# Rotary queries from two expanded tiles with mixed halves, in place of four tiles of which two are half-swapped copies

## The chip, the cores and the metric

The kernel runs on one core of a Trainium2 chip. The metric is the device time of one execution in microseconds (us). TensorE multiplies matrices, VectorE (DVE in the profile) and ScalarE (ACT) work elementwise, GpSimd (POOL) does a few elementwise steps, and SyncE (SP) issues every transfer of this kernel, in program order. PEld is TensorE's loading of a stationary operand, which overlaps the multiplication before it.

## The reference

One layer of a streaming encoder: 2048 prompt tokens and 64 sample tokens, width 1024. The part that is touched is the query side of the latent attention, with 8 heads of 64 plain and 32 rotary columns:

```
q = (rmsnorm(cq, g_q) @ w_uq).reshape(b, t, MLA_HEADS, MLA_NOPE + MLA_ROPE)
q_nope = q[..., :MLA_NOPE]
q_pe = rope(q[..., MLA_NOPE:], pos)

def rope(x, pos):            # half = 16
    x1, x2 = x[..., :half], x[..., half:]
    return jnp.concatenate([x1 * cos - x2 * sin, x1 * sin + x2 * cos], axis=-1)
```

Everything is float32. The kernel splits each operand into a high and a low part and forms three products (high by high, high by low, low by high).

## The kernel before

**Stages.** `project_inputs` comes first (to about 356 us), then window attention with the first loads of latent attention, latent attention, and the output projection with the gated feed-forward part (from about 1000 us to the end). All engines meet at the end of `project_inputs`, SyncE after its last stores have landed; the later stages overlap at their borders.

**`project_inputs`.** The 2112 tokens are cut into five blocks (`BLOCKS`) of 424 columns (the last has 416). In each block, ten weight tiles (step j = 0 to 9, chunk t = 10 b + j) are multiplied with the block's normalised input: 24 products a chunk into one of two accumulators `acc`. VectorE reads each accumulator out, times the inverse root (`product_times_rstd`), and TensorE may start chunk t when `acc_free` says that chunk t - 2 is read. Weights arrive as 512 KB transfers into three raw slots (`load_w`, L249); ScalarE makes the high part (`w_hi_of`, L412), VectorE the low part (`w_lo_of`, L546). During block b the input of block b + 1 is loaded (`load_x`, L245) and split by ScalarE (L438) and VectorE (L551).

**Expansions.** The latent vectors of block b are expanded during block b + 1, by a list: `after[j]` names the items that TensorE computes behind chunk j, and the other engines handle the same items in the same order. A block has 14 items: four of plain queries ("nope"), two of rotary queries ("rope", items 4 and 5, behind chunks 2 and 3), four of keys, four of values. Block 4's items come together at the end (`last_expansions`), then those of the old cache. Products go to four banks `ex`; `ex_done` counts products, `ex_free` counts banks that VectorE has read. The results pass through a ring of four slots; SyncE stores each slot (`keep`, L323 for values, L326 for the rest), and the slot is free when its store has landed (`ring_out`).

**A rotary item.** Item i covers four heads. TensorE expands it twice, once with its columns in order and once with the two halves of each head swapped (the host appends the swapped copy to `w_head`): 2 x 6 products. VectorE multiplies the first with the cosines and the second with the signed sines (`turn`), adds them (`turned`), and later forms the low part (`rope_low`). The eight 128-column tiles of weights for this (four by two row halves) are loaded by `more_wx(1)` in four transfers and split in one piece by `wx_hi_of(1)` and `wx_lo_of(1)`, in block 0.

**Order on SyncE around `more_wx(1)`.** In block 0 it comes behind step 4's weight load; then the rotary key, the query store (`stored`), the next weight tile, and in step 5 `keep_bias` with its eleven transfers, and the next query store. VectorE reuses a staging tile only when its query store has landed.

**Window attention.** SyncE runs a loop over 128-token tiles (`step`, L969). A step issues, in this order: the next tile's loads (L930 to L932), the spread of the reciprocals (L914), the output store (L920), a slice of values (L978), then on odd tiles `head_keys` (L954, L956) and on even tiles `head_queries` (L947, L948), which bring the first head of latent attention piece by piece, and last `keep`, the store of the reciprocals (L961). VectorE overwrites the output tile only after its store has landed (`att_out`). Tiles 4 to 11 are in a rolled loop, the others written out; tile 14 calls `head_queries` twice.

**Latent attention** loads each later head in rows of 16 (`load`, L1493).

Of the kernel before, what the change touches and what calls it, by code (L numbers as in the profile page):

```python
# [17 lines left out]
ALU = mybir.AluOpType  # L18
ACT = mybir.ActivationFunctionType
F32 = mybir.dt.float32  # L20
# [45 lines left out]
def project_inputs(nc, d, early):  # L66
# [4 lines left out]
    with ExitStack() as ctx:  # L71
# [8 lines left out]
        RING = 4  # L80
        NX = 24
        w_raw = sb("pi_w_raw", [P, RAWS, KD, P])
# [103 lines left out]
        OLD = [("old key", i) for i in range(4)] + [("old value", 0)]  # L186
        BANKS = 16
        after = [[0, 1], [2, 3], [4], [5, 6], [7], [8, 9], [10, 11], [12, 13], [], []]

        def bank(b, e):  # L190

            return BANKS * b + e + max(0, min(e - 4, 2))

# [33 lines left out]
        def _(sp):  # L227
# [46 lines left out]
            def wx(lo, hi):  # L274
                return wx_raw[:, lo:hi].rearrange("p a (h c) -> p (a h) c", h=2 if hi - lo == 4 else 4)

# [3 lines left out]
            def more_wx(part):  # L280
                sp.wait_ge(wx_split, part)
                for m in range(2 if part == 1 else 0):
                    sp.dma_start(wx(2 * m, 2 * m + 2), head_cols(m * P + NOPE, m * P + NOPE + ROPE)).then_inc(wx_in, 16)
                    sp.dma_start(wx(4 + 2 * m, 6 + 2 * m), head_cols(m * P + NOPE + ROPE, m * P + P)).then_inc(wx_in, 16)
                if part == 2:
                    sp.dma_start(wx(0, 4), head_cols(2 * P, 2 * P + NOPE)).then_inc(wx_in, 16)
                    sp.dma_start(wx(4, 8), head_cols(2 * P + NOPE, 2 * P + NOPE + V_DIM)).then_inc(wx_in, 16)
# [18 lines left out]
            def keep(b, e):  # L306

                kind, i = item(b, e)
                _, slot, _ = place(b, e)
                rows, n = width(b, e)  # L310
                if kind == "rope":
                    sp.wait_ge(turn_lo, 2 * b + i + 1)
                else:
                    sp.wait_ge(ex_free, bank(b, e) + 1)
                c0 = cols(b)[0] if b < BLOCKS else TOK
                if kind == "nope":
                    to = d["qn_scr"][i * P:(i + 1) * P, :, c0:c0 + n]
                elif kind == "rope":
                    to = d["qr_scr"][i * P:(i + 1) * P, :, c0:c0 + n]
# [84 lines left out]
        def _(act):  # L404
# [68 lines left out]
            def wx_hi_of(s):  # L473
                act.wait_ge(wx_in, (32, 96, 128)[s])
                act.activation(wx_hi[:, 8 * s:8 * s + 8], wx_raw[:], ACT.Copy).then_inc(wx_hi_made, 1)
                if s == 2:
                    act.wait_ge(old_in, 32)
                    act.activation(old_kpe[64:96, 1].bitcast(F32R), old_kpe[64:96, 0], ACT.Copy).then_inc(wx_hi_made, 1)
                    act.activation(old_hi[:], old_raw[:], ACT.Copy).then_inc(wx_hi_made, 1)
# [57 lines left out]
        def _(dve):  # L537
# [30 lines left out]
            def split_low(b, e):  # L568
# [11 lines left out]
                if kind == "rope":  # L580
                    if i == 0:
                        dve.wait_ge(rope_in[b % 2], 64 * (b // 2 + 1))
                    first = bank(b, e)
                    if 2 * b + i:
                        dve.wait_ge(turn_done, 2 * b + i)
                    for part in range(2):
                        dve.wait_ge(ex_done, first + part + 1)
                        dve.tensor_tensor(turn[:, part, 0:n], ex[:, (first + part) % 4, 0:n],
                                          rope[:, b % 2, part, 0:n], ALU.mult).then_inc(ex_free, 1)
                    if i == 1:  # L590
                        rope_low(b, 0)
# [25 lines left out]

            def wx_lo_of(s):
                dve.wait_ge(wx_hi_made, s + 1)
                dve.tensor_tensor(wx_lo[:, 8 * s:8 * s + 8], wx_raw[:], wx_hi[:, 8 * s:8 * s + 8].bitcast(F32),  # L620
                                  ALU.subtract).then_inc(wx_split, 1)
# [85 lines left out]
        def _(pe):  # L707
# [19 lines left out]
            def expand(b, e):  # L727
                kind, i = item(b, e)
                rows, n = width(b, e)
                if e == 0:  # L730
# [3 lines left out]
                    if b < BLOCKS:  # L734
                        pe.wait_ge(lat_split, 3 * b + 3)
                at = bank(b, e)
                for part in range(2 if kind == "rope" else 1):
                    if at + part >= 4:
# [4 lines left out]
                    elif kind == "rope":  # L743
                        mm = from_queries(out, 8 + 4 * part + i, 2, n)
                    elif kind == "key":
                        mm = three(out, wx_hi[:, 16 + i], wx_lo[:, 16 + i], lat_hi[:, 2, 0:n], lat_lo[:, 2, 0:n])
                    elif kind == "old key":
                        mm = three(out, wx_hi[:, 16 + i], wx_lo[:, 16 + i], old_hi[:], old_lo[:])
                    else:
                        vw_hi = wx_hi[:, 20:24].rearrange("p a c -> p (a c)")  # L750
                        vw_lo = wx_lo[:, 20:24].rearrange("p a c -> p (a c)")
                        if kind == "value":
# [53 lines left out]
def window_attention(nc, d, ahead, early, ctx, first_ctx, ps):  # L806
# [116 lines left out]
    def sync(sp, first_row):  # L923
# [301 lines left out]
def latent_attention(nc, d, ahead, mix, ctx, rooms, ps, wa, own):  # L1225
# [220 lines left out]
    def sync(sp):  # L1446
# [46 lines left out]
        def load(i, p, s):  # L1493
# [3 lines left out]
            if s in PIECE_AT:  # L1497
# [117 lines left out]
    def tensor(pe, begin):  # L1615

        def max_chunk(i, p, pos, m):
# [3 lines left out]
            if pos == 0 and m == 0:  # L1621
                pe.wait_ge(ahead["in"], 16 * 5 * 8)
                pe.wait_ge(ahead["head_in"][p], QK_DMAS * 16 * (i + 1))
# [890 lines left out]
def encoder_layer(nc, d):  # L2514
    for name, shape in (("bias_far", (P, HEADS, 2 * P)), ("qn_scr", (HEADS * NOPE, 2, TOK)), ("qr_scr", (HEADS * ROPE, 2, TOK)),
                        ("kn_scr", (HEADS * NOPE, 2, KEYS)), ("kpe_scr", (ROPE, 2, KEYS)), ("vt_scr", (KEYS, HEADS * V_DIM))):
# [172 lines left out]
```

## Time and profile before

| | us |
|---|---|
| median of 3 runs | 2764.75 |
| lowest and highest of the runs | 2761.0, 2767.46 |
| span of the profiled execution | 2765.2 |
| projections, end of the stage | about 356 |
| TensorE busy over the span | 2665.2 |
| VectorE busy over the span | 1904.3 |
| ScalarE busy over the span | 1425.0 |
| GpSimd busy over the span | 478.9 |

The profile page gives the busy time of each engine; the timeline lists instructions in order of time with the idle time before each and what ended it; the view of waits sums such idle times by waiting line and releaser. Of SyncE only the issues of transfers are listed.

### The profile page before, as it was taken

To read this page: it belongs to the slowest core of one execution; us is meant where nothing else is said; L and a number is where in the kernel's file an instruction comes from. 1 tells how busy PE (TensorE), PEld (TensorE's weight loads), DVE (VectorE), ACT (ScalarE), POOL (GpSimd) and SP (SyncE) were. 2 spreads that over 40 slices of the span, in tenths; PEclk is the share of its full clock that TensorE was granted. 3 is DMA by queue.
4 is the path that set the end of the run, shared out by engine and by line. 5 is a ranking of instruction groups with operands and counts; after the bars stand their busy time and mean duration, and the time that the engine had idled before them with its cause. 6 is when DMAs were issued, how large, how long until landed. Compare 5 with 4: busy or idle time off the path is not lost.

```text
span 2765.2 us, 45010 instructions
## 1 busy us (share of the span) xinstructions
PE 2665.2 (96%) x13603; PEld 2433.1 (88%) x13603; DVE 1904.3 (69%) x2793; ACT 1425.0 (52%) x3042; POOL 478.9 (17%) x401
## 2 busy tenths in 40 slices
PE   8999978899999998999999999999999999999997
PEld 7999844677777787999999999999999999999997
DVE  6877667788778846877478754687546875468743
ACT  5444367577666754644355443554435544356532
POOL 1111041244433441100100022000220002200001
PEclk9999999899999999999999999999999999999999
DMA  7666655444545242343334433345333443334332
GB/s 221 218 212 230 215 154 157 85 83 75 91 85 88 68 165 85 113 137 120 113 100 140 162 114 115 100 139 164 121 106 102 139 163 118 116 102 135 118 121 88
DMA packets 181775, 357.73 MB, mean 129 GB/s; under 512 B 50692, under 2 KB 119780, under 8 KB 180324
## 3 DMA queue, kind: packets, MB, share of 16 engines
q1 hardware_dynamic: 181636, 356.00, 43.7%
q8 instruction: 72, 1.18, 0.2%
q14 instruction: 67, 0.55, 0.1%
HBM read 301.28 MB, written 55.43 MB: 129 GB/s over the span
## 4 chain that ended last, share of the span: by engine, by line
PE 71%; DVE 6%; issue 3%; SPq 2%; DMA 2%; ACT 2%; POOL 1%; DVEq 0%; ACTq 0%; POOLq 0%
PE mf_acc L2214 55%; PE at_ps L1640 6%; PE at_ps L1626 2%; PE at_ps L1659 2%; PE at_ps L1662 2%; PE at_ps L1660 2%; DVE la_part L1741 1%; DVE mix_w_lo L2392 1%; DMA room<-in_w_up 1%; ACT mix_w_hi L2273 1%; DMA att_scr<-wa_outT 1%; DVE la_low L1438 1%; SPq L920 0%; SPq L914 0%; PE mf_st L2255 0%
## 5 line engine op out<-in xcount | busy, mean ns | idle before, releaser
L2392 DVE TENSOR_TENSOR mix_w_lo<-room,mix_w_hi 128x1024 fp32r<-128x1024 f32 (+1 forms) x338 | 471.3, 1395 | 528.6 <-ACT mix_w_hi L2273 527.3
L2214 PE MATMUL mf_acc<-mix_a_hi,mix_w_hi 128*128 128x424 f32 (+1 forms) x2016 | 721.2, 358 | 12.7 <-DVE mix_w_lo L2392 5.0
L2214 PE MATMUL mf_acc<-mix_a_hi,mix_w_lo 128*128 128x424 f32 (+1 forms) x2016 | 715.3, 355 | 0.0
L2214 PE MATMUL mf_acc<-mix_a_lo,mix_w_hi 128*128 128x424 f32 (+1 forms) x2016 | 713.8, 354 | 0.0
L2273 ACT ACTIVATE mix_w_hi<-room 128x1024 fp32r<-128x1024 f32 (+1 forms) x338 | 383.1, 1134 | 491.7 <-PE mf_acc L2214 479.1
L2214 PEld LDWEIGHTS mf_acc<-mix_a_hi,mix_w_hi 128*128 128x128 f32 x2016 | 379.5, 188 | 28.2 <-DVE mix_a_lo L2446 6.0
L2214 PEld LDWEIGHTS mf_acc<-mix_a_hi,mix_w_lo 128*128 128x128 f32 x2016 | 379.8, 188 | 11.3
L2214 PEld LDWEIGHTS mf_acc<-mix_a_lo,mix_w_hi 128*128 128x128 f32 x2016 | 379.8, 188 | 9.6 <-issue 0.7
L2214 PE MATMUL mf_acc<-mf_h_hi,mix_w_hi 128*128 128x424 f32 (+1 forms) x944 | 339.3, 359 | 3.0 <-DVE mf_h_lo L2483 1.4
L2214 PE MATMUL mf_acc<-mf_h_hi,mix_w_lo 128*128 128x424 f32 (+1 forms) x944 | 335.7, 356 | 0.0
L2214 PE MATMUL mf_acc<-mf_h_lo,mix_w_hi 128*128 128x424 f32 (+1 forms) x944 | 335.1, 355 | 0.0
L1640 PE MATMUL at_ps<-ahead_q,ahead_k 96*128 96x512 f32 (+8 forms) x1008 | 259.0, 366 | 0.0
L1698 ACT ACTIVATE la_prob<-at_ps 128x512 f32<-128x512 f32 (+1 forms) x336 | 175.5, 522 | 156.8 <-PE at_ps L1640 146.7
L2163 POOL TENSOR_TENSOR mf_ss<-mf_sq,mf_ss 128x424 f32<-128x424 f32 (+1 forms) x105 | 141.9, 1351 | 547.6 <-ACT mf_sq L2299 315.8
L1741 DVE TENSOR_REDUCE la_part<-at_ps 128x1 f32<-128x512 f32 (+4 forms) x328 | 188.8, 594 | 60.3 <-PE at_ps L1626 58.3
L1640 PEld LDWEIGHTS at_ps<-ahead_q,ahead_k 96*128 96x128 f32 (+2 forms) x1008 | 180.7, 192 | 37.5 <-issue 0.4
L2214 PEld LDWEIGHTS mf_acc<-mf_h_hi,mix_w_hi 128*128 128x128 f32 x944 | 178.1, 189 | 10.4 <-DVE mf_h_lo L2483 2.5
L2214 PEld LDWEIGHTS mf_acc<-mf_h_lo,mix_w_hi 128*128 128x128 f32 x944 | 178.0, 189 | 6.2 <-issue 1.7
L1438 DVE TENSOR_TENSOR la_low<-la_prob,la_high 128x512 fp32r<-128x512 f32 (+3 forms) x227 | 158.8, 706 | 33.9 <-ACT la_high L1699 29.6
L2214 PEld LDWEIGHTS mf_acc<-mf_h_hi,mix_w_lo 128*128 128x128 f32 x944 | 178.0, 189 | 4.6
L1699 ACT ACTIVATE la_high<-at_ps 128x512 fp32r<-128x512 f32 (+1 forms) x336 | 174.2, 519 | 0.0
L2464 DVE SCALAR_TENSOR_TENSOR mf_cv<-mf_u,mf_conv_w,mf_cv 128x424 f32<-128x424 f32 (+1 forms) x220 | 151.3, 688 | 32.6 <-DVE mf_cv L2461 25.7
(207 smaller groups left out, 4074.8 us busy)
## 6 DMA issues: line engine op xcount, KB each, us to landing
room<-in_w_up SPq DMA_DIRECT2D x220, 512.0 KB, 3.6
room<-in_w_down SPq DMA_DIRECT2D x80, 704.0 KB, 4.1
pi_w_raw<-in_w_in SPq DMA_DIRECT2D x49, 512.0 KB, 6.1
room<-in_w_out SPq DMA_DIRECT2D x40, 512.0 KB, 3.6
la_rec_all<-inv_scr SPq DMA_DIRECT2D x32, 256.0 KB
ahead_k<-kn_scr SPq DMA_DIRECT2D x28, 280.0 KB, 5.5
ahead_q<-qn_scr SPq DMA_DIRECT2D x28, 264.0 KB, 5.1
room<-in_x SPq DMA_DIRECT2D x4, 1696.0 KB, 11.7
```

The lines of the kernel that those rows point to most:

```text
L1438: eng.tensor_tensor(low[0:keys, x % RING, off:n], prob[0:keys, x % RAWS, off:n], high[0:keys, x % RING, off:n].bitcast(F32), ALU.subtract) ...
L1626: pe.matmul(sx[0:rows, (NCH * p + first_chunk[pos] + m) % 2, 0:n], q[0:MR, p, 0, q0:q0 + rows], k[0:MR, p, 0, c0:c0 + n], start=True, stop ...
L1640: mm = pe.matmul(out, k[0:rows, p, a, c0:c0 + keys], q[0:rows, p, b, n0 + off:n0 + n], start=(term == 0), stop=(term == 2))
L1659: pe.matmul(out, v[0:keys, p, vt, 0:V_LO.start], hi, start=(m == 0), stop=False, skip_group_check=True)
L1698: act.activation(prob[0:keys, x % RAWS, off:n], sc[0:keys, x % 4, off:n], ACT.Exp, scale=MLA_SCALE)
L1699: act.activation(high[0:keys, x % RING, off:n], sc[0:keys, x % 4, off:n], ACT.Exp, scale=MLA_SCALE).then_inc(exp_done, 1)
L1741: dve.tensor_reduce(part[0:rows, parity(p, pos), t, slot:slot + 1], sx[0:rows, bank, 0:n], AX_X, ALU.max).then_inc(sx_free, 1)
L2163: pool.tensor_tensor(ss[:, kind, 0:n], sq[:, slot, 0:n], zeros[:, 0:n] if first else ss[:, kind, 0:n], ALU.add).then_inc(sq_added, 1)
L2214: mm = pe.matmul(acc[:, t_bank[0], 0:n], w[:, g, k], x[:, k, 0:n], start=(first and k == 0 and m == 0), stop=(last and k == count - 1 and ...
L2273: act.activation(w_hi[:, g, 0:count], w_raw[:, g, 0:count], ACT.Copy).then_inc(w_hi_made, 1)
L2392: dve.tensor_tensor(w_lo[:, g, 0:count], w_raw[:, g, 0:count], w_hi[:, g, 0:count].bitcast(F32), ALU.subtract).then_inc(w_split, 1)
L2464: dve.scalar_tensor_tensor(out=out, in0=u[:, g, 1:n + 1], scalar=conv_w[:, 1, bass.ds(f, 1)], in1=out, op0=ALU.mult, op1=ALU.add).then_inc ...
```

## The change

The two halves x1 and x2 of each head's rotary columns are laid into two tiles. Tile A holds x1 of the even heads and x2 of the odd heads; tile B holds x2 of the even heads and x1 of the odd heads. Each has 8 heads by 16 rows = 128 rows. With C the cosines and S the signed sines (minus for even heads' rows, plus for odd ones'), A C + B S is the first half of the even heads' result and the second half of the odd heads'; B C - A S is the other. So item 4 computes both tiles (2 x 6 products, behind chunk 2), item 5 computes none on TensorE, and VectorE multiplies the same two banks again for item 5; the banks are freed then. What else changes with it:

- `more_wx(1)` issues eight transfers of 16-column pieces of four heads in place of four of 32-column pieces of eight heads; 4 weight tiles are split in place of 8 (`WX`, `NX`).
- `BANKS`, the number of banks a block uses, is 14 in place of 16.
- `qr_scr` is laid out by halves. `head_queries` therefore issues two transfers for the rotary rows (16 rows each) in place of one (32 rows), eight more in all; the later heads' loads keep their number and size.

```diff
-        NX = 24
+        NX = 20
+        WX = ((0, 8), (8, 12), (12, 20))
...
-            return BANKS * b + e + max(0, min(e - 4, 2))
+            return BANKS * b + e
...
+            def half_turns(m, tile, odd):
+
+                at = m * P + NOPE + (ROPE // 2 if tile != odd else 0)
+                to = wx_raw[:, 2 * tile + m].rearrange("p (h e c) -> p h e c", e=2, c=ROPE // 2)[:, :, odd]
+                return to, d["w_head"][odd::2, :, at:at + ROPE // 2].rearrange("h p c -> p h c")
...
                 for m in range(2 if part == 1 else 0):
-                    sp.dma_start(wx(2 * m, 2 * m + 2), head_cols(m * P + NOPE, m * P + NOPE + ROPE)).then_inc(wx_in, 16)
-                    sp.dma_start(wx(4 + 2 * m, 6 + 2 * m), head_cols(m * P + NOPE + ROPE, m * P + P)).then_inc(wx_in, 16)
+                    for tile in range(2):
+                        for odd in range(2):
+                            sp.dma_start(*half_turns(m, tile, odd)).then_inc(wx_in, 16)
...
             def wx_hi_of(s):
-                act.wait_ge(wx_in, (32, 96, 128)[s])
-                act.activation(wx_hi[:, 8 * s:8 * s + 8], wx_raw[:], ACT.Copy).then_inc(wx_hi_made, 1)
+                a, z = WX[s]
+                act.wait_ge(wx_in, (32, 160, 192)[s])
+                act.activation(wx_hi[:, a:z], wx_raw[:, 0:z - a], ACT.Copy).then_inc(wx_hi_made, 1)
...
-                    first = bank(b, e)
+                    first = bank(b, 4)
...
-                    for part in range(2):
-                        dve.wait_ge(ex_done, first + part + 1)
-                        dve.tensor_tensor(turn[:, part, 0:n], ex[:, (first + part) % 4, 0:n],
-                                          rope[:, b % 2, part, 0:n], ALU.mult).then_inc(ex_free, 1)
+                    for half in range(2):
+                        part = half ^ i
+                        dve.wait_ge(ex_done, first + half + 1)
+                        dve.tensor_tensor(turn[:, part, 0:n], ex[:, (first + half) % 4, 0:n],
+                                          rope[:, b % 2, part, 0:n], ALU.mult).then_inc(ex_free if i else turn_parts, 1)
                     if i == 1:
                         rope_low(b, 0)
-                    dve.wait_ge(ex_free, first + 2)
+                        dve.wait_ge(ex_free, first + 2)
+                    else:
+                        dve.wait_ge(turn_parts, 2 * b + 2)
                     dve.tensor_tensor(turned[:, i, 0:n], turn[:, 0, 0:n], turn[:, 1, 0:n],
-                                      ALU.add).then_inc(turn_done, 1)
+                                      ALU.subtract if i else ALU.add).then_inc(turn_done, 1)
...
+                if kind == "rope" and i == 1:
+                    return
...
-                        mm = from_queries(out, 8 + 4 * part + i, 2, n)
+                        mm = from_queries(out, 8 + 2 * part, 1, n)
...
-            sp.dma_start(ahead["q"][NOPE:NOPE + ROPE, 0, :, cols].bitcast(F32),
-                         d["qr_scr"][0:ROPE, :, cols]).then_inc(ahead["in"], 16)
+            for e in range(2):
+                rows = slice(NOPE + ROPE // 2 * e, NOPE + ROPE // 2 * (e + 1))
+                sp.dma_start(ahead["q"][rows, 0, :, cols].bitcast(F32),
+                             d["qr_scr"][e, 0:ROPE // 2, :, cols]).then_inc(ahead["in"], 16)
...
-                                 d["qr_scr"][bass.ds(h * ROPE, ROPE)][r:r + 16]).then_inc(ahead["head_in"][g], 16)
+                                 d["qr_scr"][(m - 4) ^ g, bass.ds(j * ROPE, ROPE)][g * 16:g * 16 + 16]).then_inc(ahead["head_in"][g], 16)
```

The remaining lines of the diff renumber the key and value tiles, the stores' targets and the counts that TensorE waits for.

## Rows read from the trace of the kernel before

**Rows 1.** The page: span, and busy time of each engine
```profile
span 2765.2 us, 45010 instructions
PE 2665.2 (96%) x13603; PEld 2433.1 (88%) x13603; DVE 1904.3 (69%) x2793; ACT 1425.0 (52%) x3042; POOL 478.9 (17%) x401
```

**Rows 2.** Windows: length, busy us of PE, PEld, DVE, ACT, POOL, clock, DMA share, GB/s
```profile
0.00:356.00 356.00, 336.91 (x1645) 309.57 (x1645) 254.24 (x320) 147.56 (x243) 39.76 (x36) 0.98 0.67 220
356.00:500.00 144.00, 111.76 (x705) 66.00 (x705) 105.96 (x195) 107.94 (x373) 44.66 (x33) 0.97 0.52 143
```

**Rows 3.** Timeline of TensorE, block 1: start us, length us, instruction
```profile
94.56 0.35 PE L716 MATMUL pi_ex<-pi_lat_hi,pi_wx_hi 128*128 128x424 f32 x1
...
96.86 0.35 PE L774 MATMUL pi_acc<-pi_x_hi,pi_w_hi 128*128 128x424 f32 x1
```

**Rows 4.** Waits of VectorE, 99 to 286 us: us in total, times, longest
```profile
DVE pi_w_lo L546 <- ACT pi_w_hi L412: 33.1, 13, 5.0
...
DVE pi_stage L635 <- PE pi_acc L774: 0.2, 1, 0.2
```

**Rows 5.** Waits of ScalarE, 99 to 286 us
```profile
ACT pi_w_hi L412 <- DMA pi_w_raw<-in_w_in: 69.9, 15, 8.7
...
ACT pi_x_hi L438 <- DMA room<-in_x: 6.7, 2, 3.4
```

**Rows 6.** Timeline: reads of chunks 29, 39, then starts of 31, 41
```profile
207.38 0.59 DVE L635 TENSOR_TENSOR pi_stage<-pi_acc,pi_rstd 128x424 f32<-128x424 f32 x1
...
209.50 0.19 PEld L774 LDWEIGHTS pi_acc<-pi_x_hi,pi_w_hi 128*128 128x128 f32 x1
...
272.13 0.59 DVE L635 TENSOR_TENSOR pi_stage<-pi_acc,pi_rstd 128x424 f32<-128x424 f32 x1
...
272.89 0.19 PEld L774 LDWEIGHTS pi_acc<-pi_x_hi,pi_w_hi 128*128 128x128 f32 x1 [0.15 <-issue]
```

**Rows 7.** Timelines of VectorE and ScalarE, block 4 and its end
```profile
305.57 0.59 DVE L635 TENSOR_TENSOR pi_stage<-pi_acc,pi_rstd 128x416 f32<-128x416 f32 x1 [1.28 <-PE pi_acc L774]
...
335.38 0.52 ACT L461 ACTIVATE pi_ring<-pi_ex 128x416 fp32r<-128x416 f32 x1 [3.02 <-DMA vt_scr<-pi_ring]
```

**Rows 8.** Timelines of SyncE and VectorE in block 0
```profile
46.51 0.38 SPq L283 DMA_DIRECT2D pi_ring<-in_w_head  x1
...
48.18 1.37 SPq L284 DMA_DIRECT2D pi_ring<-in_w_head  x1
49.59 0.58 SPq L365 DMA_DIRECT2D out_kpe<-pi_kp  x1
51.23 0.35 SPq L378 DMA_DIRECT2D q_scr<-pi_stage  x1
51.62 0.43 SPq L249 DMA_DIRECT2D pi_w_raw<-in_w_in  x1
...
67.88 0.60 DVE L635 TENSOR_TENSOR pi_stage<-pi_acc,pi_rstd 128x424 f32<-128x424 f32 x1 [2.76 <-DMA q_scr<-pi_stage]
```

**Rows 9.** SyncE in window attention: timeline, last row its wait for GpSimd
```profile
395.45 0.67 SPq L948 DMA_DIRECT2D ahead_q<-qr_scr  x1
396.43 0.30 SPq L961 DMA_DIRECT2D rec_scr<-wa_rec_rows  x1
...
462.12 0.65 SPq L948 DMA_DIRECT2D ahead_q<-qr_scr  x1
463.78 0.30 SPq L961 DMA_DIRECT2D rec_scr<-wa_rec_rows  x1
...
478.07 0.61 SPq L948 DMA_DIRECT2D ahead_q<-qr_scr  x1
478.73 0.48 SPq L961 DMA_DIRECT2D rec_scr<-wa_rec_rows  x1
...
483.77 1.68 SPq L978 DMA_DIRECT2D ahead_v<-vt_scr  x1
...
SPq L920 <- POOL wa_outT L1051: 4.7, 1, 4.7
```

More of the change, by code:

```diff
@@ L186, in project_inputs @@
         OLD = [("old key", i) for i in range(4)] + [("old value", 0)]
-        BANKS = 16
+        BANKS = 14
         after = [[0, 1], [2, 3], [4], [5, 6], [7], [8, 9], [10, 11], [12, 13], [], []]
         def bank(b, e):
-            return BANKS * b + e + max(0, min(e - 4, 2))
+            return BANKS * b + e
         def expansions(b, j, one):
@@ L274, in wx @@
             def wx(lo, hi):
-                return wx_raw[:, lo:hi].rearrange("p a (h c) -> p (a h) c", h=2 if hi - lo == 4 else 4)
+                return wx_raw[:, lo:hi].rearrange("p a (h c) -> p (a h) c", h=2)
+            def half_turns(m, tile, odd):
+                at = m * P + NOPE + (ROPE // 2 if tile != odd else 0)
+                to = wx_raw[:, 2 * tile + m].rearrange("p (h e c) -> p h e c", e=2, c=ROPE // 2)[:, :, odd]
+                return to, d["w_head"][odd::2, :, at:at + ROPE // 2].rearrange("h p c -> p h c")
             for m in range(2):
@@ L318, in keep @@
                 elif kind == "rope":
-                    to = d["qr_scr"][i * P:(i + 1) * P, :, c0:c0 + n]
+                    to = d["qr_scr"][i, :, :, c0:c0 + n]
                 elif kind in ("key", "old key"):
@@ L618, in wx_lo_of @@
             def wx_lo_of(s):
+                a, z = WX[s]
                 dve.wait_ge(wx_hi_made, s + 1)
-                dve.tensor_tensor(wx_lo[:, 8 * s:8 * s + 8], wx_raw[:], wx_hi[:, 8 * s:8 * s + 8].bitcast(F32),
+                dve.tensor_tensor(wx_lo[:, a:z], wx_raw[:, 0:z - a], wx_hi[:, a:z].bitcast(F32),
                                   ALU.subtract).then_inc(wx_split, 1)
@@ L743, in expand @@
                     elif kind == "rope":
-                        mm = from_queries(out, 8 + 4 * part + i, 2, n)
+                        mm = from_queries(out, 8 + 2 * part, 1, n)
                     elif kind == "key":
-                        mm = three(out, wx_hi[:, 16 + i], wx_lo[:, 16 + i], lat_hi[:, 2, 0:n], lat_lo[:, 2, 0:n])
+                        mm = three(out, wx_hi[:, 12 + i], wx_lo[:, 12 + i], lat_hi[:, 2, 0:n], lat_lo[:, 2, 0:n])
                     elif kind == "old key":
-                        mm = three(out, wx_hi[:, 16 + i], wx_lo[:, 16 + i], old_hi[:], old_lo[:])
+                        mm = three(out, wx_hi[:, 12 + i], wx_lo[:, 12 + i], old_hi[:], old_lo[:])
                     else:
-                        vw_hi = wx_hi[:, 20:24].rearrange("p a c -> p (a c)")
-                        vw_lo = wx_lo[:, 20:24].rearrange("p a c -> p (a c)")
+                        vw_hi = wx_hi[:, 16:20].rearrange("p a c -> p (a c)")
+                        vw_lo = wx_lo[:, 16:20].rearrange("p a c -> p (a c)")
                         if kind == "value":
@@ L1621, in max_chunk @@
             if pos == 0 and m == 0:
-                pe.wait_ge(ahead["in"], 16 * 5 * 8)
+                pe.wait_ge(ahead["in"], 16 * 6 * 8)
                 pe.wait_ge(ahead["head_in"][p], QK_DMAS * 16 * (i + 1))
@@ L2514, in encoder_layer @@
 def encoder_layer(nc, d):
-    for name, shape in (("bias_far", (P, HEADS, 2 * P)), ("qn_scr", (HEADS * NOPE, 2, TOK)), ("qr_scr", (HEADS * ROPE, 2, TOK)),
+    for name, shape in (("bias_far", (P, HEADS, 2 * P)), ("qn_scr", (HEADS * NOPE, 2, TOK)), ("qr_scr", (2, HEADS * ROPE // 2, 2, TOK)),
                         ("kn_scr", (HEADS * NOPE, 2, KEYS)), ("kpe_scr", (ROPE, 2, KEYS)), ("vt_scr", (KEYS, HEADS * V_DIM))):
```

## The prediction

> **What bounds the kernel.** I read the page first. The span is 2765.2 us and TensorE is marked busy for 96% of it [rows 1]; a busy share says little of what one product is worth, so I split the span by stage. The projection stage, where the change sits, ends near 356 us with its weight loads busy for 309.57 us of that; in the stage behind it, to about 500 us, they are busy for 66.00 of 144 us [rows 2]. In the first stage TensorE looks like the bound, in the second it is not.
>
> The price of a product comes from TensorE's timeline. The twelve products of one rotary group start at 94.56 us and the next work starts at 96.86 us: 2.30 us for twelve, 0.192 us each [rows 3]. The change takes twelve from each of the five blocks, so the naive gain is 5 x 2.30 = 11.5 us (0.4%). Where does it arrive? That needs the waits, and there a second view decides.
>
> From 99 to 286 us (blocks 1 to 3 and the start of block 4) VectorE waits for TensorE once, for 0.2 us. Its other idle time, 33.1 us of it, ends with ScalarE's weight halves, and ScalarE waits 69.9 us for the weight transfers and 6.7 us for the x transfer [rows 4, 5]. So beside TensorE's chain there runs a second one that TensorE does not drive: x lands, ScalarE and VectorE split it, VectorE does its share of the old block's expansions, the value rows go out, the weight transfers behind them on the queue land late, the next x is issued late. TensorE is coupled to it through `acc_free`: chunk t needs the product of chunk t - 2 read. I took the margin where the block begins. At chunk 31 VectorE's read ends at 207.97 and the chunk starts at 209.50: 1.53 us. At chunk 41 it ends at 272.72 and the chunk starts at 272.89, after an idle of 0.15: nothing is left [rows 6]. The two chains are equally long here. I read this pair because a busy share or a missing wait on one engine can't show how near the other chain is; the difference of two ends can.
>
> **The change, part by part.** (a) Expansions of blocks 0 to 2, at step 3 of blocks 1 to 3. TensorE reaches chunks 14, 24 and 34 earlier by 2.30 us, up to 6.9 us in sum. VectorE's work is the same in number and shape (four multiplications, two sums or differences, two low halves a block), in the same steps, and its first half-tile is ready no sooner than before, because both tiles are now multiplied out at step 2, where one group was. Chunk 41 still waits for the read that ends at 272.72. I therefore count 0.2 us, the one wait on TensorE that can move [rows 4], and keep 6.9 us as the other end. Banks are no new wait: the two tiles are now held until the second pair of multiplications, at step 3, and the next product into one of their banks is made at step 5.
>
> (b) Expansion of block 3, in block 4. There is no next x to split, VectorE has room, and it waits 1.28 us for TensorE at 305.57. Behind this wait come the value rows, and ScalarE's last row of plain queries at 335.38 waits 3.02 us for a store of values to land [rows 7]. So the end of the stage moves with that wait, by 1.3 us at most along this path and by 2.3 at most in all. I take 1.3; the lower end is 0.
>
> (c) Expansion of block 4, at the very end. From 335.38 on ScalarE, VectorE and the stores set the pace and the rotary products are made before their readers are free. I take 0, with 2.3 as the bound.
>
> (d) Loading the rotary weights: eight transfers of 16-column pieces where there were four of 32. SyncE issues the old four from 46.51 to 49.55 (the first takes 0.38 us, the last 1.37), then the key store, 0.58 us, to 50.17, and then waits until 51.23 anyway, 1.06 us [rows 8]. Four more, between the 0.43 us of the weight load and the 0.58 of the key store, with 0.04 between two issues, are 1.9 to 2.5 us; less the spare 1.06, and less up to 0.8 if the long issue falls away. This gives 0 to 1.5 us; I take 0.7. It is on the path: what follows on the queue is the bias and the query store whose landing VectorE awaits for 2.76 us at 67.88, and TensorE awaits VectorE [rows 8]. The split of the 4 tiles instead of 8 saves some 0.6 us each on ScalarE and VectorE, hidden under this same wait.
>
> (e) The early load of the first head's queries in window attention: each of eight calls issues three transfers where there were two. An issue takes 0.67 us, and 0.18 us of address arithmetic stand before it (the old one ends at 396.12 after starting at 395.45). In the rolled loop the next instruction on the queue, the reciprocals' store, starts at 396.43: 0.31 us to spare. So each of the four calls there costs 0.85 - 0.31 = 0.54 us, 2.2 us in sum. The call at 462.12 ends 1.0 us before its store at 463.78, and hides its 0.69. The double call that ends at 478.68 is followed at 478.73 with no gap: two issues of 0.65 are 1.3 us [rows 9]. The first call is hidden: SyncE waits 4.7 us for GpSimd after it [rows 9]. Behind the store stand the loads, the spread and the output store, on whose landing VectorE waits to free its tile, so this queue is the loop. I take +3.5 us, with 0 as the lower end and 7 x 0.85 = 6.0 as the upper.
>
> The Trainium skill speaks to this term (DMA: Bandwidth & Descriptors, "Issuing engines are not separate DMA queues"): the time a sequencer takes to initiate a transfer is usually small relative to the transfer. By that rule the term (e) would be 0 and the sum below -0.8. The rows of this case speak against it: an issue of 0.67 us there sits in a queue with 0.31 us to spare.
>
> (f) The later head loads have the same count and size; only their rows differ. Nothing is taken.
>
> **The sum.** -0.2 - 1.3 + 0 + 0.7 + 3.5 = +2.7 us on the profiled execution's span of 2765.2 us, thus 2767.9. The median shown, 2764.75, lies 0.45 us below that execution, so I forecast 2767.5 us: no difference that this measurement tells from none, which I put at 0.2%, or 5.5 us.
>
> **The rivals.** R1, TensorE is the bound through the projections: chunk 41's lack of margin would be a chance of this one execution. For: weight loads are busy 309.57 of 356 us [rows 2]. Against: the margin of chunk 31 is 1.53 us too, below one block's saving. Time: -9.2 (four blocks; the tail stays) + 0.7 + 3.5 = -5.0, 2759.8 us. R2, the added issues are hidden in window attention, because the loop's real length is set by VectorE and the landing of the output stores: -0.2 - 1.3 + 0.7 = -0.8, 2764.0 us. For: in the step of 462.12 the queue does have 1.0 us to spare. Against: the four rolled steps have 0.31 and the double call none [rows 9]. This is also where the rule of the Trainium skill cited under (e) would end. R3, both: -8.5, 2756.3 us. R4, the slower side: the issues in window attention block on a fuller queue. One issue of this stretch takes 1.68 us, at 483.77, after the double call [rows 9]. If each of the seven late calls costs that, less the gaps (4 x 0.31 and 1.0), it is 11.8 - 2.2 = 9.5 us instead of 3.5; with the rest, +8.7, 2773.5 us. It decides once an added issue takes over 1.2 us.
>
> **Chances and range.** Forecast 0.50, R1 0.18, R2 0.12, R3 0.06, R4 0.14. R1 lies on the edge of 0.2%, so half of it counts as faster; of the forecast I give 0.08 to slower, since the bounds of (d) and (e) add to 3.3 us. Faster 0.09 + 0.06 = 0.15; slower 0.14 + 0.08 = 0.22; same 0.63. The range leaves out R3, and R4 beyond its near end: 2759 to 2771.5 us.
>
> **What would show it.** Right: 60 matmuls fewer into `pi_ex`, 20 on each of the three lines of `three`; in blocks 2 to 4 TensorE has new idle before chunks, ended by VectorE's reads (about 2 us a block); the x transfers of blocks 2 to 4 land at the same distance as before; the projection stage ends within 1.5 us of its old end; window attention grows by 3 to 4 us. Wrong: a stage that ends 8 us earlier with no new idle (R1), a window stage of unchanged length (R2), issues of over a microsecond behind the third transfer (R4). What I could not see is how the queue answers 64-byte pieces; a slower landing there would push (d) above its bound.

## The result, and the profile of the changed kernel

The changed kernel takes 2767.64 us in the median of 20 runs (2762.69 to 2773.76), the kernel before 2762.95 us in 20 runs beside it (2758.86 to 2767.46). The ratio is 1.0019, 95% interval 1.0013 to 1.0026: slower by 4.7 us between the medians, by the interval 3.6 to 7.2 us. The sign is clear; the size lies at the edge of the 0.2% (5.5 us) that the prediction named as no difference, and the interval reaches beyond it. Forecast were 2767.5 us and a difference of +2.7 us.

The page of the changed kernel (span 2765.8 us), beside [rows 1], and its first window, beside [rows 2]:

```profile
PE 2652.8 (96%) x13543; PEld 2420.8 (88%) x13543; DVE 1904.5 (69%) x2793; ACT 1425.0 (52%) x3042; POOL 476.8 (17%) x401
```

```profile
0.00:356.00 356.00, 327.83 (x1601) 299.68 (x1601) 254.86 (x323) 148.34 (x244) 39.68 (x41) 0.97 0.67 220
```

In the first 356 us TensorE is busy 9.1 us less than in [rows 2] (327.83 and 336.91 us), and 8.5 us less in a second pair of profiles (328.61 and 337.07). Over the whole span the difference is 12.4 us in the first pair and only 1.3 us in the second (2660.5 and 2661.8), so the sum over the span is no measure of what was saved. The span is 0.6 us longer all the same. The groups of expansions show the sixty products that are gone. The first of the three lines is shown; each of the three has 80 where there were 100:

```profile
L729 PE MATMUL pi_ex<-pi_lat_hi,pi_wx_hi x80: 348/355/684, 79.6 to 336.8; 128*128 128x424 f32 x64, 128*128 128x416 f32 x16
```

Where did the 2.3 us a block go? The waits of TensorE from 99 to 286 us (total, times, longest; DVEq is VectorE's instruction queue). The kernel before has none of them in its first profile and one of 0.6 us in its second:

```profile
PE pi_acc L789 <- DVEq L692: 3.4, 3, 1.8
PE pi_acc L789 <- DVE pi_w_lo L555: 1.1, 1, 1.1
```

And two places, chunk 26 and chunk 41, in the timelines of VectorE and TensorE (start, length, instruction, idle before it and what ended it; the low half before chunk 41 starts at 269.94, after 3.85 us of idle that ScalarE's high half ends):

```profile
175.37 1.38 DVE L555 TENSOR_TENSOR pi_w_lo<-pi_w_raw,pi_w_hi 128x1024 fp32r<-128x1024 f32 x1 [0.67 <-ACT pi_w_hi L420]
176.67 0.58 DVE L648 TENSOR_TENSOR pi_stage<-pi_acc,pi_rstd 128x424 f32<-128x424 f32 x1
...
271.08 0.59 DVE L648 TENSOR_TENSOR pi_stage<-pi_acc,pi_rstd 128x424 f32<-128x424 f32 x1
```

```profile
177.43 0.19 PEld L789 LDWEIGHTS pi_acc<-pi_x_hi,pi_w_hi 128*128 128x128 f32 x1 [2.14 <-DVE pi_w_lo L555]
...
271.84 0.19 PEld L789 LDWEIGHTS pi_acc<-pi_x_hi,pi_w_hi 128*128 128x128 f32 x1 [0.63 <-DVE pi_w_lo L555]
```

The reader is to see the order on VectorE. The read of the accumulator that TensorE needs stands behind a low half of a weight tile, and that stood waiting for ScalarE's high half, which waited for its transfer. The releaser named is `pi_w_lo`, whose semaphore TensorE also waits on; but the chunk starts 0.18 us after the end of the accumulator's read, at 177.25, and 0.17 us after the other, at 271.67. In [rows 6] chunk 31 had 1.53 us there. In the changed kernel the chunks 20, 21, 26, 28, 30, 36, 40 and 41 start 0.1 to 0.2 us after the read of the chunk two before them; in the kernel before, from chunk 11 on, only chunk 41 does (in its second profile 40 and 41), and the distances at 20, 26, 30 and 40 are 2.37, 2.13, 0.72 and 1.34 us. The two chains were nearly equally long; now TensorE's is the shorter one, by about what was taken from it.

What the whole program did is best told by two stages. P runs from TensorE's first weight load of chunk 4, behind the start-up, to SyncE's first issue of window attention; W from there to the fifteenth pair of output stores. Chunk 41 cuts P. All are starts from the timelines of TensorE and SyncE, in us:

| kernel | chunk 4 | to chunk 41 | from there to the end of P | P | W |
|---|---|---|---|---|---|
| before | 42.28 | 230.61 | 83.78 | 314.39 | 140.48 |
| before, second profile (e9) | 42.24 | 230.86 | 83.76 | 314.62 | 140.28 |
| changed | 41.15 | 230.70 | 82.16 | 312.86 | 145.46 |
| changed, second profile (e10) | 41.89 | 230.18 | 81.77 | 311.95 | 145.21 |

P is 2.1 us shorter in the mean and W 5.0 us longer. In W the queue of SyncE, around the rotary transfers of [rows 9], reads:

```profile
410.71 1.49 SPq L965 DMA_DIRECT2D ahead_q<-qr_scr  x2
...
478.20 1.28 SPq L965 DMA_DIRECT2D ahead_q<-qr_scr  x2
479.53 0.60 SPq L962 DMA_DIRECT2D ahead_q<-qn_scr  x1
```

There are two issues where there was one, back to back. What comes next starts 0.13 us after their end in the first place (the reciprocals' store, at 412.33) and 0.05 us after it in the second.

### The profile page after: what moved, and what is told of

It is laid out like the page before. It is cut to its first block, busy times and chain, and to the rows that moved or that the text cites. A ratio compares the mean times of both kernels' runs of the same rounds, so it can differ in the third digit from the quotient of the medians.

```text
span 2765.8 us, 44910 instructions
## 1 busy us (share of the span) xinstructions
PE 2652.8 (96%) x13543; PEld 2420.8 (88%) x13543; DVE 1904.5 (69%) x2793; ACT 1425.0 (52%) x3042; POOL 476.8 (17%) x401
## 4 chain that ended last, share of the span: by engine, by line
PE 71%; DVE 5%; issue 3%; SPq 3%; DMA 2%; ACT 2%; POOL 1%; DVEq 0%; ACTq 0%; POOLq 0%
PE mf_acc L2231 55%; PE at_ps L1657 6%; PE at_ps L1643 2%; PE at_ps L1676 2%; PE at_ps L1679 2%; PE at_ps L1677 2%; DVE mix_w_lo L2409 1%; DMA room<-in_w_up 1%; DVE la_part L1758 1%; ACT mix_w_hi L2290 1%; SPq L935 1%; DVE la_low L1455 0%; SPq L929 0%; DMA room<-in_w_out 0%; DMA att_scr<-wa_outT 0%
## 5 line engine op out<-in xcount | busy, mean ns | idle before, releaser
L2231 PE MATMUL mf_acc<-mix_a_hi,mix_w_hi 128*128 128x424 f32 (+1 forms) x2016 | 719.9, 357 | 14.7 <-DVE mix_w_lo L2409 7.5
## 6 DMA issues: line engine op xcount, KB each, us to landing
room<-in_x SPq DMA_DIRECT2D x4, 1696.0 KB, 12.4
```

The source lines that it names most:

```text
L2231: mm = pe.matmul(acc[:, t_bank[0], 0:n], w[:, g, k], x[:, k, 0:n], start=(first and k == 0 and m == 0), stop=(last and k == count - 1 and ...
```

## Experiments

Each was timed against the kernel before on the same chip.

**e1: the added issues alone, in the kernel before.**

```diff
-            sp.dma_start(ahead["q"][NOPE:NOPE + ROPE, 0, :, cols].bitcast(F32),
-                         d["qr_scr"][0:ROPE, :, cols]).then_inc(ahead["in"], 16)
+            for e in range(2):
+                rows = slice(ROPE // 2 * e, ROPE // 2 * (e + 1))
+                sp.dma_start(ahead["q"][NOPE + rows.start:NOPE + rows.stop, 0, :, cols].bitcast(F32),
+                             d["qr_scr"][rows, :, cols]).then_inc(ahead["in"], 16)
```

> The kernel before, with one edit: in window attention the rotary rows of the first head come in two transfers of 16 rows where there was one of 32, eight issues more in all. Theory (the issues on SyncE's queue are the whole loss): window attention 4 to 5 us longer, from the sum of my step (e), 3.5 us, and from the 5.0 us by which the stage grew in the profile after; time +3.5 to +5 us, ratio 1.0013 to 1.0018, and the gap between the third and the fourth store of the rolled loop's second half also grows. Rival (the loss lies elsewhere, in the later heads' loads or in the rotary weights): +1 us or less, ratio within 0.0004 of 1. Rival of the fuller queue: single issues above 1.2 us and +8 us or more.

2768.56 us against 2764.05, ratio 1.0016 (1.0008 to 1.0025): +4.5 us, as expected. W is 145.18 us, as in the changed kernel (145.46, 145.21), and P is 315.36. The eight issues explain the length of W by themselves, and nothing else of the change is needed for it. No issue takes over 1.2 us in the rolled part, so it is not the fuller queue. One part of the expectation failed: the step that grew by 1.8 us in the changed kernel (below) does not stand out here.

**e2: one transfer in the changed kernel, reading two separate pieces.**

```diff
-            for e in range(2):
-                rows = slice(NOPE + ROPE // 2 * e, NOPE + ROPE // 2 * (e + 1))
-                sp.dma_start(ahead["q"][rows, 0, :, cols].bitcast(F32),
-                             d["qr_scr"][e, 0:ROPE // 2, :, cols]).then_inc(ahead["in"], 16)
+            sp.dma_start(ahead["q"][NOPE:NOPE + ROPE, 0, :, cols].bitcast(F32),
+                         d["qr_scr"][:, 0:ROPE // 2, :, cols]).then_inc(ahead["in"], 16)
```

> The changed kernel, with its two transfers of 16 rotary rows put back into one transfer of 32 rows that reads both halves from their two places. Theory: window attention is as long as in the kernel before; what is left is what the projections gained, from the two profiles -0.3 (blocks 1 to 3), -1.6 (block 4), +0.4 (rotary weights), sum -1.5 us against the kernel before, ratio 0.9993 to 0.9997. Rival (later loads of heads cost something too): +1 us or more against the kernel before, ratio above 1.0003, and latent attention longer than before by about that. Rival (TensorE was the bound after all and the profile after was an odd one): -6 us or more, ratio 0.998.

A miss: 2769.85 us, ratio 1.0019 (1.0010 to 1.0028), and W is 146.52 us in its one profile, longer than with two issues. (The times do not tell the two apart: the changed kernel's ratio is 1.0019 as well.) My reading of W as a matter of issue time alone would have been refuted here, had the profile not shown a new wait. SyncE's waits from 380 to 500 us:

```profile
SPq L929 <- DMA rec_scr<-wa_rec_rows: 6.8, 7, 1.5
```

In the changed kernel the same row has 0.9 us, once. The queue of e2 shows where the wait stands, and a window of it the load of the 16 DMA engines (the last two numbers are their mean busy share and GB/s):

```profile
411.08 0.79 SPq L963 DMA_DIRECT2D ahead_q<-qr_scr  x1
412.09 0.31 SPq L976 DMA_DIRECT2D rec_scr<-wa_rec_rows  x1
...
413.91 0.38 SPq L947 DMA_DIRECT2D room<-v_scr  x1
415.85 1.17 SPq L929 DMA_DIRECT2D wa_rec_all<-rec_scr  x2
```

```profile
412.50:414.00 1.50, 1.33 (x9) 0.98 (x9) 1.50 (x4) 1.25 (x3) 0.00 (x0) 1.00 0.13 26
```

From 414.29 to 415.85 SyncE stands still. The reciprocals' store, 4 KB, was issued behind the combined transfer and lands late, and the spread must wait for it. The plain transfer of the same 66 KB lands in 2.4 us in the kernel before. The landing of the combined one is not in the trace, but behind its issue the 16 engines are busy for 0.13 of the time, which is 2.1 of them. e6 below keeps count and size and changes the shape alone. The Trainium skill (DMA: Bandwidth & Descriptors, "Why a DMA increments its semaphore by 16 and not by 1") says that a transfer is shared by the largest number of engines up to 16 that divides the slowest dimension of both its sides, which would be 2 engines here and 16 for the plain transfer of 32 rows. The share of 2.1 of 16 in this window agrees with the 2.

**e6: the same with a plain transfer.** One transfer of 32 adjacent rows, `d["qr_scr"][0, 0:ROPE, :, cols]`. The second halves of head 0 are left out, and rows of another head stand in their place.

> The changed kernel, with one transfer of 32 adjacent rows for the first head's rotary rows (rows 0 to 31 of the first half alone: the second half of head 0 is left out and rows of another head stand in its place), so that count, shape and size of the transfers are those of the kernel before. e2, whose single transfer read two separate pieces, left window attention 6 us longer and showed a new wait of SyncE for the landing of the reciprocals' store, 6.8 us in 7 times. Theory (that transfer's shape did it, and with a plain transfer the loss is gone): window attention within 0.6 us of the kernel before, the wait for the reciprocals' store at most 1 us, time -1 to -2.5 us against the kernel before, ratio 0.9991 to 0.9997. Rival (another part of the change lengthens window attention): it stays 4 us or more longer, ratio 1.0015.

W is 141.02 us, 0.6 above the kernel before, P is 311.56, and SyncE waits 0.9 us once for the reciprocals' store: the theory of the stage holds, it was the shape in e2. The time is 2764.4 us, ratio 1.0005 (0.9996 to 1.0013), above the expected 0.9991 to 0.9997, though the intervals touch.

**e3: the products alone, in the kernel before.** Each rotary expansion is made of three products in place of six; the left out ones are those with the low parts of the latent vectors and one with low weights.

```diff
-                        mm = from_queries(out, 8 + 4 * part + i, 2, n)
+                        at_w = 8 + 4 * part + i
+                        pe.matmul(out, wx_hi[:, at_w], lat_hi[:, 0, 0:n], start=True, stop=False)
+                        pe.matmul(out, wx_lo[:, at_w], lat_hi[:, 0, 0:n], start=False, stop=False)
+                        mm = pe.matmul(out, wx_hi[:, at_w + 2], lat_hi[:, 1, 0:n], start=False, stop=True)
```

> The kernel before, with three products in place of six for each of the four rotary expansions of a block (the products of low parts of the latent vectors and one of low weights are left out): 12 products fewer a block, as in the change, and nothing else changed. Theory (a second chain through x, the splits and the transfers bounds blocks 1 to 3): the projection stage ends 1.5 to 2.5 us earlier and not 9 to 11.5; time -1.5 to -2.5 us, ratio 0.9991 to 0.9995; TensorE idles about 2 us a block more, ended by VectorE's reads. Rival (TensorE is the bound): -9 us or more, ratio 0.9967 or less, no new idle.

2761.31 us, ratio 0.9994 (0.9985 to 1.0002). P is 312.24, 2.3 us below the two profiles of before; TensorE as the bound would have given 9 or more. Sixty products fewer, without anything else of the change, give the same 2 us. The new idle of TensorE is less than expected: 4.6 us over the three blocks, 1.5 us a block, where about 2 were forecast.

**e4 and e5: the second chain made shorter, in the kernel before and in the changed one.** The value stores of blocks 0 to 3 have 106 rows. They are cut into 96 and 10, and the waits of the ring count both.

```diff
+                    full = rows if rows != 106 else 96
-                    sp.dma_start(d["vt_scr"][c0 + i * rows:c0 + (i + 1) * rows],
-                                 ring[0:rows, slot, 0, 0:n].bitcast(F32)).then_inc(ring_out[slot], 16)
+                    sp.dma_start(d["vt_scr"][c0 + i * rows:c0 + i * rows + full],
+                                 ring[0:full, slot, 0, 0:n].bitcast(F32)).then_inc(ring_out[slot], 16)
+                    if full != rows:
+                        sp.dma_start(d["vt_scr"][c0 + i * rows + full:c0 + (i + 1) * rows],
+                                     ring[full:rows, slot, 0, 0:n].bitcast(F32)).then_inc(ring_out[slot], 16)
```

> The kernel before, with each value store of blocks 0 to 3 (106 rows of 2 KB, which takes long to land and holds the weight transfers behind it) issued as two stores, of 96 rows and of 10. Theory (blocks 1 to 3 have two chains of nearly equal length, and the stores belong to the second): the weight transfers land earlier behind the stores, but TensorE's own chain holds the pace, so little is gained: 0 to -2 us. Rival (the stores are not what makes the weights late): no landing changes, and 16 issues more at 0.4 us cost up to 2 us.

> The changed kernel, with the same split of the value stores. Theory: with the second chain shortened the 2.3 us a block that TensorE saves arrive: 2 to 7 us less than the changed kernel, which makes it equal to or up to 3 us faster than the kernel before (ratio 0.999 to 1.0005), and the difference between this kernel and the one before with the same split is smaller than +4.7 us by 2 to 6 us. Rival (something other than the stores holds the second chain, or the savings vanish behind the end of the stage): as the changed kernel, ratio 1.0015 to 1.0025.

e4: 2762.63 us against 2765.33, ratio 0.9996 (0.9987 to 1.0005), P 312.61. e5: 2758.42 us, ratio 0.9976 (0.9967 to 0.9985), P 303.54. The same edit is worth 1.9 us of P where TensorE has its old work, and 8.9 us where it has the new. Read the other way: with the value stores cut, the change is worth 9.1 us of P (312.61 and 303.54), close to the 9.2 us at which R1 priced four blocks, and 2.1 us without the cut. This is the surest answer to where the expected gain went: it was there, 2.3 us a block, behind the stores. The distance from the read to the start of chunks 31 and 41, 1.53 and 0.17 us in the kernel before, is 5.86 and 5.82 us in e4 and 4.98 and 4.62 in e5.

How the stores hold the chain shows on SyncE's own queue. In the changed kernel, behind two value stores:

```profile
134.99 6.19 SPq L250 DMA_DIRECT2D pi_w_raw<-in_w_in  x1
```

```profile
135.00:141.00 6.00, 5.89 (x31) 5.29 (x30) 3.12 (x6) 0.28 (x1) 1.22 (x1) 1.00 0.13 52
```

The issue of one weight transfer takes 6.19 us, and in that time the 16 DMA engines have a busy share of 0.13, which is 2.1 of them. The same place takes 6.18 and 6.32 us in the two blocks that follow (in the kernel before, 3.52 and 4.59 us on two issues in a row). In e5 no single issue of a weight transfer between 99 and 286 us takes over 2 us, and from 133 to 141 us the share is 0.85. Transfers issued from 99 to 286 us, in the changed kernel and then in e5 (count, KB each, median us to landing):

```profile
pi_w_raw<-in_w_in SPq DMA_DIRECT2D x30, 512.0 KB, 8.0
...
room<-in_x SPq DMA_DIRECT2D x2, 1696.0 KB, 14.7
```

```profile
pi_w_raw<-in_w_in SPq DMA_DIRECT2D x30, 512.0 KB, 5.3
...
room<-in_x SPq DMA_DIRECT2D x2, 1696.0 KB, 10.2
```

The largest transfers, none of which was touched, land 2.7 and 4.5 us sooner when the value stores are cut. x lands at 159.78 and 223.71 in the changed kernel, 63.9 us apart, and at 151.12 and 211.03 in e5, 59.9 apart. Chunk 31 to chunk 41 takes 63.6 us in the changed kernel and 60.9 in e5. VectorE's read before chunk 41 no longer stands behind a late weight: it ends at 261.01, and chunk 41 starts at 265.64. e4 came out as expected (0 to 2 us less; P is 1.9 us shorter). For e5 I had expected 2 to 7 us below the changed kernel, too little: the ratios differ by 0.0043, 12 us, of which P gives 8.9.

**e7 and e8: the second halves in one late transfer,** without and with the cut stores. The first halves come piece by piece; the second halves of all columns (16 rows, 264 KB) are issued once, in the step of tile 12.

```diff
+            if isinstance(t, int) and t == NT - 4:
+                sp.dma_start(ahead["q"][NOPE + ROPE // 2:NOPE + ROPE, 0].bitcast(F32),
+                             d["qr_scr"][1, 0:ROPE // 2]).then_inc(ahead["in"], 16)
```

> The changed kernel; in window attention the first halves come piece by piece as before, the second halves of all columns in one transfer of 16 rows in the step of tile 12, where SyncE waited 1.0 us anyway: one added issue in place of eight. Theory: window attention at most 1 us longer than in the kernel before, time -0.5 to -2 us against it, ratio 0.9993 to 0.9999. Rival (the large transfer, 264 KB, holds up the output stores behind it on the queues): 2 us or more are lost at tile 12, ratio 1.000 to 1.001.

> The changed kernel with both repairs: the value stores of blocks 0 to 3 split into 96 and 10 rows, and the second halves in one late transfer. Theory: the two add up, -6.9 us (measured with the first alone) and another -3.5 to -4.5 us: -10 to -12 us against the kernel before, ratio 0.9957 to 0.9964. Rival (they share their gain, since the later stages give part of it back): -7 to -9 us, ratio 0.997.

e7: 2765.34 us against 2762.52, ratio 1.0011 (1.0003 to 1.0020); W 142.21, 1.8 us above the kernel before, where at most 1 was expected. The rival had the place right, and its ratio of 1.000 to 1.001 nearly. The late transfer was issued at 464.12 and landed at 468.48, 4.36 us later. SyncE's waits from 385 to 500 us:

```profile
SPq L929 <- DMA rec_scr<-wa_rec_rows: 2.6, 2, 1.7
```

It is e2's wait again. Its P was 314.43 in this one profile, 2 us more than in the others of the changed kernel. e8: 2754.63 us in five runs, ratio 0.9965 (0.9953 to 0.9978), 7.9 us below the kernel before by the medians; P 303.09, W 142.64. That is less than the 10 to 12 us expected, and what its rival said (7 to 9).

**e9 and e10: both kernels unchanged, a second profile.**

> The kernel before, unchanged, for a second profile of its stages. From the fifth chunk of the projections to the first issue of window attention it took 314.4 us in its first profile and 315.4 us in e1; from there to the fifteenth output store 140.5 us. If stages repeat as well as the times do, both come again within 1 us.

> The changed kernel, unchanged, for a second profile. The stages of the first profile (projections 1.5 us shorter, window attention 5.0 longer, and what other versions of it show) sum to about +3 us, while the times say +4.7 us (interval 3.6 to 7.2). Theory A (the projections now have no margin in either chain, and take over the variation of the transfers): the stage lies anywhere between 311.5 and 314.5 us in single profiles, with a mean gain nearer 1 than 2 us. Theory B (a stage behind window attention is 1 to 2 us longer): from the fifteenth output store to the end it takes 2 us more than before, where the first profiles show 2268.1 us before and 2266.4 after. Time as before: ratio 1.0010 to 1.0026.

The changed kernel: 2767.23 us against 2762.42, ratio 1.0019 (1.0010 to 1.0028), the first result again. The stages are in the table above; those of the kernel before came again within 0.3 us, as expected. Neither theory on the changed kernel is borne out: P is 311.95, no smaller gain than the first time, and from the fifteenth output store to the end it takes 2266.6 us, against 2265.6 in the second profile of before and 2268.1 and 2266.4 in the first ones.

**e11 and e12: the late transfer moved to the last step,** without and with the cut stores (`t == NT` in place of `t == NT - 4`).

> As e7, with the one transfer of the second halves moved from the step of tile 12, where the reciprocals' store landed behind it and SyncE waited 1.7 us for that, to the last step, where SyncE waits 2.5 us for VectorE anyway. Theory: window attention within 0.7 us of the kernel before; time -2 to +1 us against it (ratio 0.9993 to 1.0004), 1 to 2 us less than e7. Rival (latent attention starts later, since it waits for this last transfer, 4.4 us to land): the start of latent attention's first products moves back by up to 2 us and the time is that of e7.

> The changed kernel with the split value stores and the second halves in one transfer in the last step. Theory: the gains add, the time is 1 to 2 us below e8, ratio 0.9955 to 0.9965 against the kernel before. Rival (as e11): as e8, 0.9965.

e11: 2766.91 us, ratio 1.0014 (1.0005 to 1.0023). W is 141.06, as expected, but the time is not. The rival was right. The late transfer is issued at 488.72 and lands at 492.92, and the first product of latent attention that reads the queries starts behind 4.67 us of idle that this landing ends:

```profile
493.16 0.77 PE L1644 MATMUL at_ps<-ahead_k,ahead_q 112*128 112x128 f32 x2 [4.67 <-DMA ahead_q<-qr_scr]
```

In the kernel before that product starts 5.0 us before the fifteenth output store, here 1.0 us before it. The first product of scores starts 6.2 us after that store, in e7 4.0 us and in the kernel before 3.3. e12 missed its expectation too: 2756.20 us, ratio 0.9976 (0.9967 to 0.9985), P 303.42, W 141.14, no better than e8, whose interval it overlaps; e8 stays the fastest version, by the median.

## Why the prediction was right

The time was inside the range and 0.1 us from the forecast, and that it came so near is luck: the forecast started from a median of before that the further runs put 1.8 us lower, and its terms erred in both directions. In differences: +2.7 forecast, +4.7 measured (3.6 to 7.2), +2.9 by the stages of the two pairs of profiles. "No difference" was the right side of the bound by a hair; by its interval it is a small loss. What was right is the mechanism: a second chain takes the saved products, and the added issues set the sign.

- **(a), and the choice of the second chain: right, and shown.** Forecast for blocks 1 to 3 and the rotary weights together, -0.2 + 0.7 = +0.5 us up to chunk 41; measured 230.4 against 230.7 in the means, -0.3. The margins of [rows 6] carried this: e3 reproduces it without the rest of the change (chunk 41 comes 1.5 us earlier, of 6.9 saved), and e5 shortens the second chain and finds the gain (6.9 us earlier). One profile is a thin ground for such a margin: chunk 31 has 1.53 us in the first and 0.24 in the second.
- **(b) and (c): right in path, a little small.** Forecast -1.3 and 0, measured -1.6 and -2.0 behind chunk 41, within the bound of 2.3 that (b) named. Counted from chunk 41, the row of plain queries before ScalarE's last one starts 2.3 us earlier, and the landing of a value store takes 0.7 of it back, since the last row waits 3.68 us where it waited 3.02 [rows 7]:

```profile
332.68 0.52 ACT L469 ACTIVATE pi_ring<-pi_ex 128x416 fp32r<-128x416 f32 x1 [3.68 <-DMA vt_scr<-pi_ring]
```

- **(d): not shown apart from nothing.** Chunk 4 to chunk 9 takes 26.38 and 25.84 us before, 26.78 and 26.33 after: +0.45, forecast +0.7 within 0 to 1.5. But e1 and e4, which load these weights as before, take 26.85 and 25.90, and e2 and e6, which load them the new way, 26.20 and 26.23.
- **(e): the mechanism right (e1), the size too small:** +3.5 forecast, +5.0 measured, within the 6.0 of its upper end. Of it the rolled loop has 3.7 us where 2.2 stood. Its four steps take 8.19, 7.90, 7.89 and 7.94 us from one output store to the next before, and 8.77, 8.57, 9.72 and 8.59 after. Three of them grew by 0.58 to 0.67, a little over the 0.54 forecast, since 0.1 us or more of the gap behind the transfers stays. The third in order grew by 1.8, and holds a single long issue, which comes at the same place in the second profile too (1.39 us), and neither in the kernel before nor in e1:

```profile
431.76 1.51 SPq L947 DMA_DIRECT2D room<-v_scr  x1
```

  What makes it long is not shown. The written-out steps grew by 1.3, as much as the double call was priced at; in which of them it arises differs between the two pairs of profiles.
- **The rivals.** R1 (TensorE is the bound) falls with the idle before chunks 26 and 41 and with e3; R2 (issues hidden) with e1, where eight issues of 0.59 to 0.68 us cost 4.5 us; R4 with the added issues, which all take 0.59 to 0.67 us. The Trainium skill (DMA: Bandwidth & Descriptors, "Issuing engines are not separate DMA queues") calls the time to initiate a transfer usually small relative to the transfer; here it is 0.6 to 0.7 us for transfers of 33 KB that land in 2.2, and what the prediction drew from the rule, a term (e) of 0, does not hold. (The sum without (e) is -0.8, not below it.)
- **The signs.** Of those the prediction named, the sixty matmuls and the x transfers came: the last two land 63.7 us apart before and 63.9 after, the two before them 69.5 and 68.0. The new idle was 4.7 us over the three blocks, 1.6 a block where about 2 were named. Two missed: window attention grew by 5.0 us, not 3 to 4, and the projection stage ended 2.7 and 3.0 us earlier, not within 1.5; of this P gives 1.5 and 2.7 and the start-up the rest.

**What stays open.** The profiles' stages sum to +2.9 us, the times say at least 3.6. In e6 and e11 the time lies about 4 us above what their stages give (P, W, and in e11 the later start) and in e2 2.4 us, while e1, e3, e4, e5, e7, e8 and e12 agree with theirs within 1.3 us. A stage comes from one execution and a time from many. The two profiled spans of the kernel before, 2765.2 and 2762.7 us, are 4.0 and 2.1 us longer than its median runs (a span is 1.8 us shorter than the device time of the same run), those of the changed kernel within 0.3 us of its median; and e6's profiled run, 2759.33 us, is 5.1 us faster than its median. That is as large as what is missing. Behind W, single profiles of all kernels scatter by several microseconds (2263.1 us in e6, 2269.6 in e5), so a difference of 1 to 2 us there cannot be told from them. One more thing on record goes with the gap: the mean granted clock of TensorE over a kernel's runs is 0.984 to 0.985 in the changed kernel, e2, e6 and e11, and 0.986 in the runs of the kernel before beside them and in e3, e4, e5, e8 and e12, whose stages and times agree; e7, with 0.985, agrees too. Whether the clock costs the missing time, and what lowers it, no run shows.

## What to carry over

Before counting a saved product as time, take the distance between the two chains that meet at a buffer, where each block begins: here it was 2.0, 1.5 and 0.2 us at chunks 21, 31 and 41, each less than one block's saving of 2.3, and busy shares of 96% and an engine without waits hid it. A gain that vanishes this way is not lost: shorten the other chain, and both edits pay together (in P 2.1 us and 1.9 us alone, 11.0 us together). In a queue that paces a loop, count issues before bytes, and look at what small store lands behind a large or badly shaped transfer.

## What was unexpected of the hardware

- A store of 106 rows of 2 KB delays transfers that were issued behind it and around it: with 96 + 10 rows the 512 KB weights land in 5.3 us where it was 8.0, the 1696 KB of x in 10.2 where it was 14.7, at the price of one more issue for each store. By the rule of the Trainium skill cited under e2 (DMA: Bandwidth & Descriptors, "Why a DMA increments its semaphore by 16 and not by 1"), 106 rows go to 2 engines, 96 to 16 and 10 to 10; the trace agrees with the 2, with a share of 2.1 of 16 behind two such stores, and does not count the others.
- Behind such stores SyncE's issue of the next transfer itself took 6.2 to 6.3 us, where issues of weight transfers otherwise take 0.4 to 0.6 us in most places. The engine that issues stood still with the queue.
- One transfer with an outer dimension of two cost the loop more than two transfers (W 146.5 us in one profile against 145.5 and 145.2; the times do not differ), through the landing of a 4 KB store behind it.
- A late transfer of 264 KB took 4.36 us to land, and SyncE waited 1.7 us for the same small store behind it.
